# Order of work at the ends of two mixer stages, and one program segment in place of two

## The reference, cut to what matters

```
for layer in range(2):
    m = hybrid_mixer(x, w_in[layer], ...)            # convolution branch and delta-rule branch, then @ w_out
    x = layer_norm(ALPHA * x + m, ln_mix_g[layer], ln_mix_b[layer])
    f = swiglu(x, gate, up, down) if layer == 0 else moe_swiglu(x, router_w, ...)
    x = layer_norm(ALPHA * x + f, ln_ffn_g[layer], ln_ffn_b[layer])
```

## Time and profile before

| what | value |
|---|---|
| median of 3 runs (lowest, highest) | 2788.82 us (2786.13, 2789.67) |
| the profiled execution, its span | 2790.31 us, 2788.1 us |
| PE busy in the span | 2613.4 us, 94% |
| DVE, ACT busy | 1857.6 us (67%), 1341.6 us (48%) |
| share of PE in the chain that ended last | 79% |
| mixA, dense | about 1051 to 1283, 1284 to 1477 us of the span |
| mixB, experts | about 1479 to 1727, from 1728 us |

### The profile page before, as it was taken

The page is one execution under the profiler, slowest core; times in us unless marked ns, Lnnn a source line. Parts: engine busy times, 40 slices in busy tenths (PEclk is TensorE's granted clock), DMA queues, the critical chain, the costliest instruction groups (busy, mean ns, idle before and its releaser), DMA issues.

```text
span 2788.1 us, 35704 instructions
## 1 busy us (share of the span) xinstructions
PE 2613.4 (94%) x14582; PEld 2210.1 (79%) x14582; DVE 1857.6 (67%) x2155; ACT 1341.6 (48%) x1414; POOL 0.2 (0%) x4
## 2 busy tenths in 40 slices
PE   6999999999999999968999976999999999999896
PEld 6889689898986998846997854877787878787775
DVE  6664354576634545845446855888888888888786
ACT  4554144455414433213332213766766767676663
POOL 0000000000000000000000000000000000000000
PEclk9999999999999999988999987999999999999999
DMA  5334355343344544105443204999999999999795
GB/s 222 121 122 148 142 211 194 117 150 119 122 164 184 188 171 142 47 31 196 181 166 125 76 16 152 357 348 336 348 342 348 343 339 352 342 349 344 289 348 219
DMA packets 119314, 593.15 MB, mean 213 GB/s; under 512 B 17392, under 2 KB 17648, under 8 KB 77040
## 3 DMA queue, kind: packets, MB, share of 16 engines
q1 hardware_dynamic: 109920, 585.40, 56.7%
q10 hardware_dynamic: 9232, 5.47, 0.7%
HBM read 589.79 MB, written 1.05 MB: 212 GB/s over the span
## 4 chain that ended last, share of the span: by engine, by line
PE 79%; DVE 12%; ACT 5%; issue 3%; DMA 1%; DVEq 0%; POOLq 0%; ACTq 0%; SPq 0%
PE bank L2355 29%; PE bank L555 19%; PE bank L786 8%; PE bank L1567 6%; PE bank L1034 3%; PE bank L1048 2%; ACT whi L629 2%; DVE ring_lo L762 1%; PE bank L1777 1%; PE bank L1757 1%; PE bank L2313 1%; PE bank L2335 1%; ACT slot_hi L756 1%; DVE wlo L634 1%; PE bank L1587 1%
## 5 line engine op out<-in xcount | busy, mean ns | idle before, releaser
L634 DVE TENSOR_TENSOR wlo<-ring,whi 128x2048 fp32r<-128x2048 f32 x428 | 979.5, 2291 | 203.0 <-ACT whi L629 197.4
L629 ACT ACTIVATE whi<-ring 128x2048 fp32r<-128x2048 f32 x433 | 828.1, 1913 | 273.2 <-PE bank L2355 139.4
L2355 PE MATMUL bank<-whi,xhi 128*128 128x512 f32 x896 | 362.0, 404 | 8.9 <-DVE wlo L634 6.9
L2355 PE MATMUL bank<-whi,xlo 128*128 128x512 f32 x896 | 352.2, 393 | 0.0
L2355 PE MATMUL bank<-wlo,xhi 128*128 128x512 f32 x896 | 350.3, 391 | 0.0
L762 DVE TENSOR_TENSOR ring_lo<-ring,slot_hi 128x1024 fp32r<-128x1024 f32 x128 | 155.1, 1224 | 151.2 <-ACT slot_hi L756 144.0
L555 PE MATMUL bank<-xhi,whi 128*128 128x256 f32 x864 | 246.0, 285 | 9.3 <-POOLq L2651 8.1
L555 PE MATMUL bank<-xlo,whi 128*128 128x256 f32 x864 | 245.8, 285 | 0.0
L555 PE MATMUL bank<-xhi,wlo 128*128 128x256 f32 x864 | 245.8, 285 | 0.0
L786 PE MATMUL bank<-xh,slot_hi 128*128 128x256 f32 x704 | 202.1, 287 | 3.0 <-DVE ring_lo L762 3.0
L2355 PEld LDWEIGHTS bank<-whi,xhi 128*128 128x128 f32 x896 | 168.9, 189 | 41.3 <-DVE wlo L634 7.3
(11 more groups left out here) (455 smaller groups left out, 4347.3 us busy)
## 6 DMA issues: line engine op xcount, KB each, us to landing
ring<-in_stream SPq DMA_DIRECT2D x555, 1024.0 KB, 6.2
par<-in_par ACTq DMA_DIRECT2D x2, 2048.0 KB, 9.9
con<-in_con SPq DMA_DIRECT2D x1, 1280.0 KB, 8.6
X<-in_x SPq DMA_DIRECT2D x1, 1024.0 KB, 5.0
out_y<-X SPq DMA_DIRECT2D x1, 1024.0 KB, 4.0
par<-in_par ACTq DMA_DIRECT2D x2, 448.0 KB, 5.9
par<-in_par ACTq DMA_DIRECT2D x2, 157.5 KB, 3.4
gains<-in_par ACTq DMA_DIRECT2D x2, 16.0 KB, 4.9
```

Source lines behind the costliest of these rows:

```text
L629: act.activation(whi[:, k % NSPLIT, :], src, ACT.Copy).then_inc(act_done, AC.step(tag + f".w{k}"))
L634: v.tensor_tensor(wlo[:, k % NSPLIT, :], src, whi[:, k % NSPLIT, :].bitcast(F32), ALU.subtract)\
L2355: mm = pe.matmul(out, left, right, start=start and i == 0, stop=stop and i == len(pairs) - 1)
```

## The change

Four edits. `turned` uses bank 2 in place of 1. In both mixers the gating `y` on DVE comes before the splits of slots 0 and 1 of the next stage. mixA and dense become one segment of 49 slots: the segment end between them is gone, the swiglu's slots 0 to 32 are slots 16 to 48 of mixA, and their first two splits count in `slots_split`. `t_ffn3` is given `turn="An2"`, so that `first_up` waits block by block. The gain and the bias on X move from the start of dense into its loop: the gain after split 5, the bias after split 8.

```
-AHEAD = {"dense": 2, "moe": NSPLIT - 1}
+AHEAD = {"moe": NSPLIT - 1}
-            segs += [("mixA", SLOTS_MIX2, 1), ("dense", SLOTS_DENSE, 1), ("mixB", SLOTS_MIX2, 1),
+            segs += [("mixA", SLOTS_MIX2 + SLOTS_DENSE, 1), ("mixB", SLOTS_MIX2, 1),
-            return {..., "dense": 0, "moe": 0, "over": 0}.get(tag, n_slots[tag])
+            return {..., "mixA": SLOTS_MIX2, "moe": 0, "over": 0}.get(tag, n_slots[tag])
-            return PS[(1, 3, 4, 5)[k // 2]][:, (k % 2) * T:(k % 2 + 1) * T]
+            return PS[(2, 3, 4, 5)[k // 2]][:, (k % 2) * T:(k % 2 + 1) * T]
...
         def v_ffn3(v, tag, units, gated, rg_, first, wide=None):
                 if k < n:
                     v_split(v, tag, k, rg_)
+                if wide is not None:
+                    wide(k)
...
         def mix_scalar(act, tag, layer, last):
-            rga.start("moe" if last else "dense", 0)
+            if last:
+                rga.start("moe", 0)
+            else:
+                rga.start("mixA", 0)
+                rga.k = SLOTS_MIX2
             for k in range(2):
-                a_split(act, tag + "next", k, rga)
+                a_split(act, tag + "next" if last else "fd", k, rga)
...
         def mix_vector(v, tag, layer, last):
             normed(1)
-            for k in range(2):
-                v_split_ahead(v, tag + "next", k)
             ... (y)
+            if last:
+                for k in range(2):
+                    v_split_ahead(v, tag + "next", k)
+            else:
+                rgv.start("mixA", 0)
+                rgv.k = SLOTS_MIX2
+                for k in range(2):
+                    v_split(v, "fd", k, rgv)
...
         def second_tensor(pe):
+            def first(it):
+                mix_tensor(pe, "A", 0, False)
+                t_ffn3(pe, "fd", UNITS_DENSE, True, 0, "An2")
                 t_turn(pe, "fdn", X)
+            for_segment(eng, "mixA", 1, first)
...
         def second_vector(v):
+                def wide(k):
+                    if k == 5:
+                        v.wait_ge(wide_loaded, 16)
+                    if k in (5, 8):
+                        op, y = (ALU.mult, p2("lnmg")) if k == 5 else (ALU.add, p2("lnmb"))
+                        v_wait(v)
+                        for t in range(NT):
+                            v.tensor_tensor(X[:, t, :], X[:, t, :], y, op).then_inc(vec_done, VE.step())
+
+                v_ffn3(v, "fd", UNITS_DENSE, True, rgv, 2, wide)
```

More of the change, by code:

```diff
@@ L261, in split_from @@
         def split_from(tag):
-            return {L1[0]: PROJ1 + 10, L1[1]: PROJ1 + 10, "dense": 0, "moe": 0, "over": 0}.get(tag, n_slots[tag])
+            return {L1[0]: PROJ1 + 10, L1[1]: PROJ1 + 10, "mixA": SLOTS_MIX2, "moe": 0, "over": 0}.get(tag, n_slots[tag])
         class Ring:
@@ L665, in a_ffn3, with v_ffn3 @@
                        .then_inc(act_done, AC.step(tag + f".hh{u}"))
-        def v_ffn3(v, tag, units, gated, rg_, first):
+        def v_ffn3(v, tag, units, gated, rg_, first, wide=None):
             after, later = split_order(units, gated)
@@ L2543, in second_tensor @@
             eng = ("pe", pe, PE, pe_done)
-            for_segment(eng, "mixA", 1, lambda it: mix_tensor(pe, "A", 0, False))
-            def dense(it):
-                t_ffn3(pe, "fd", UNITS_DENSE, True, AHEAD["dense"])
+            def first(it):
+                mix_tensor(pe, "A", 0, False)
+                t_ffn3(pe, "fd", UNITS_DENSE, True, 0, "An2")
                 t_turn(pe, "fdn", X)
-            for_segment(eng, "dense", 1, dense)
+            for_segment(eng, "mixA", 1, first)
             for_segment(eng, "mixB", 1, lambda it: mix_tensor(pe, "B", 1, True))
@@ L2561, in second_scalar, with first @@
             eng = ("act", act, AC, act_done)
[L2562 to L2567, removed]
+            def first(it):
+                mix_scalar(act, "A", 0, False)
+                a_ffn3(act, "fd", UNITS_DENSE, True, rga, 2)
                 for t in range(NT):
@@ L2586, in second_vector, with first @@
             eng = ("vec", v, VE, vec_done)
[L2587 to L2598, removed]
+            def first(it):
+                mix_vector(v, "A", 0, False)
+                def wide(k):
[7 more added lines that the diff above has]
+                v_ffn3(v, "fd", UNITS_DENSE, True, rgv, 2, wide)
                 def down_done(t, f):
```

## The result

The changed kernel takes 2759.3 us (median of 4, 2758.1 to 2761.8) against 2789.1 us before (4 runs): ratio 0.9894, 95% interval 0.9882 to 0.9906. Timed again beside the first experiments it took 2762.2 (5 runs, 2759.2 to 2765.3): ratio 0.991 (0.9896 to 0.9923). The forecast, 2761.2, lies between the two medians, and the change takes away 26 to 30 us.

What follows compares the result with a forecast made beforehand. PE bounds the kernel, busy 94% of the span. 10.3 + 6.9 + 10.4 = 27.6 us off 2790.3 gives 2762.7; the median of the runs lies 1.5 under the profiled execution, so 2761.2. Range 2756.5 to 2768.

Steps and rivals of the forecast that it cites:

- The gating: End of both mixers: gating ahead of the splits shortens PE's wait by 8.1 us in the first, 8.3 in the second.
- The charge of 0 for DVE's late first add: Output product of both mixers: DVE's first add comes 1.0 and 3.3 us late but catches up, costing 0.
- the bound of 3.3 us: Second mixer's output product: the most DVE's late first add could cost, its whole lateness, 3.3 us.
- The clock behind it: Output product after the gating: PE's clock stays full over the shorter gap, gaining 2.2 us in the first mixer, 2.1 second.
- the rival of a fall there: Both mixers: the clock falls at the gating too, taking back 2.2 + 2.1 us, giving 2765.5; chance 0.17.
- The swiglu's start: Ahead of the swiglu: without the segment end PE starts when the first block is ready, gaining 6.9 us.
- the half one: First 16 products of the swiglu: the clock is taken to be at half, gain 0.
- the 1.6 us that the prediction kept as the other end: Swiglu's start: rival that the clock holds at full, 1.6 us more, giving 2759.6; chance 0.22.
- the rule weighed in the prediction: Transposes don't count as busy PE for the clock; sides with half clock at the swiglu's start after 5.3 us, not certain.
- Gain and bias: Moved on DVE from the head of dense to behind splits 5 and 8: covered, 0; without cover 4.7 us.
- second mixer's six loads behind the last split: Second mixer's start: six loads are issued some 5 us later, still before PE needs them; 0, other end 5 us.
- counted as shifted alike: Stages between and behind the changed places shift as a whole, with no gain or loss of their own.

Runs made afterwards that it cites:

- the first experiments: Four kernels timed on one chip: changed kernel again 2762.2 us, kernel before with only the gating reordered 2767.7, changed kernel with old order in first mixer 2760.4, in second 2769.4.
- the filler kernels: Changed kernel plus identity products on PE whose results nothing reads, at the swiglu's start and in most also at other places; medians 2747.3 to 2760.4 us.
- the one and two products at its head: Changed kernel with unused products at the swiglu's start, plus one or two at the second mixer's head to start it later: 2760.4 and 2757.7 us.

## Why the prediction was right

**The gating.** Confirmed term by term: 8.18 and 8.35 us of wait for 8.1 and 8.3, and, by the order alone, 20.5 of 20.7 in both mixers. The charge of 0 for DVE's late first add held; the bound of 3.3 us wasn't touched, the fourth add waiting 1.44 us for PE. What the prediction did not say is that in the first mixer the joined segment would have done it without the order.

**The clock behind it.** Right in size, 2.17 and 2.11 for 2.2 and 2.1. With a gap of 1.5 us PE kept 1.00, and L1779's like took 14.00 us in both mixers of every trace with the gap, so the rival of a fall there is out for this kernel.

**The swiglu's start.** 6.86 for 6.9, of which 6.4 is the start by blocks. Of the two clocks the half one came, as chosen, in all eight profiles without filler, the kernel before's among them; in the six with filler it was the full one, so the 1.6 us that the prediction kept as the other end were there to be had. The transposes are on PE between L1779 and the first product in all of them; with them alone the clock fell at 1265.0, with three more products among them it didn't. This agrees with the rule weighed in the prediction (the Trainium skill, "TensorE: Matmul & The Clock Gate", Part 4: PE-mode transpose), but does not prove it: the fillers also made PE busier by 2.6 us. Nor did transposes alone always mean a fall: of the first block's two layers, with 4.4 us of transposes and waits where the swiglu has 5.4, the first started at half clock and the second at full before, and the other way round after, by the same instructions.

**Covers.** Gain and bias: 0, and 0.4 at the old place, where the prediction gave 4.7 for no cover at all. Bank, loads, second mixer's six loads behind the last split: 0.

**What it missed**, 1.9 us, lies in stages that it counted as shifted alike, and most of it came before the first changed place. The rows there point to the clock: L1736 took 2.35 us before and its like 1.99 after. The prediction had put 2 us on that; the filler kernels show that the same stage can differ by 5. That the median came within 2 us of the forecast is therefore partly luck; the terms read from the traces aren't.

## What to carry to other kernels

Ask of each instruction ahead of an urgent one on its queue not only how long it takes but what it waits for: 4.6 us of splits cost 8 us a mixer only because the second waited for a load, and with the load early they cost nothing in the same place. PE's idle time has a second price behind it, the clock: here a gap of 9.7 us cost 2.2 us more, and idle work put into waits of 2 to 4.8 us gained another 12 us in all. The rows at the filled places account for 8 of them (6.6 in the mixers, 1.5 at the swiglu's start); the rest hangs on where the clock's falls came to lie. Since a shift of 2 us in one stage can move a later one by 5, read a small edit from its own stretch of the trace, and not from the total.

## What the runs showed of the hardware that was not expected

The second mixer's stretch, the same instructions with DVE busy 129.3 us in all, took 175.4, 177.6 (no start by blocks) or 180.5 us, in step with the mean granted clock of 0.96 to 0.93. Which it is changed with when it started, as the one and two products at its head show (180.2 and 175.3). What fixes the falls' moments relative to the kernel's start is not settled by these runs. Even the first block, the same in all kernels, started its second layer's feed-forward at full clock in one trace and at half in another.

Filler did nothing where it outlasted the wait: behind the router three products ran at half clock, 5.5 us in a wait of 3.6, and the 1 us that PE was earlier at the experts was lost in their stage.
